# Mask and row maximum in one VectorE instruction, softmax weights scaled on VectorE, and two short query blocks in one PSUM bank, in the attention of the second of two transformer blocks

## What is computed

```python
def one_block(args):                       # one block of 128 queries
    ...
    score = jnp.where(admissible[None], score.astype(jnp.float32), -jnp.inf)
    _, sel = lax.top_k(score, k_sel)       # 128 keys for each query
    ...
    logits = (jnp.einsum('bqhr,bqkr->bqhk', ql, c_sel) * scale
              + jnp.swapaxes(bias, -1, -2))
    logits = jnp.where(valid[:, :, None, :], logits, -jnp.inf)
    p = jax.nn.softmax(logits, axis=-1)
    return jnp.einsum('bqhk,bqkr->bqhr', p, c_sel)
...
y = jnp.einsum('bsc,cd->bsd', jnp.concatenate([o_a, o_b], axis=-1), w_o)
x = _layer_norm(DEEPNORM_ALPHA * x + y, ln_g, ln_b)
```

## Time and profile before

| what | value |
|---|---|
| median of three runs | 1611.55 us (1610.61 to 1613.72) |
| the profiled execution | 1609.34 us, span of its instructions 1608.0 us |
| PE busy | 1540.8 us, 96% of the span |
| DVE, ACT, POOL busy | 992.7, 678.1, 194.0 us |
| mean granted TensorE clock | 0.985 |
| chain that ended last, by engine | PE 82%, DVE 9%, ACT 6%, POOL 2% |

### The profile page before, as it was taken

One profiled execution on the slowest core, in us unless ns is written; L12 is line 12 of the kernel. 1 busy time (PEld: TensorE's weight loads), 2 busy tenths in 40 slices (PEclk: granted clock), 3 DMA queues, 4 the chain that ended last, 5 costly groups with the idle time before them and its releaser, 6 DMA issues.

```text
span 1608.0 us, 18855 instructions
## 1 busy us (share of the span) xinstructions
PE 1540.8 (96%) x7486; PEld 1252.0 (78%) x7486; DVE 992.7 (62%) x1556; ACT 678.1 (42%) x1142; POOL 194.0 (12%) x176
## 2 busy tenths in 40 slices
PE   8999999999999999999989999999999998999797
PEld 6777878888888888677758888888888867886574
DVE  7466667966666656677764644434344489896444
ACT  6444444513232335455553522323243454556533
POOL 0000002000000012111103000000002005665211
PEclk9998999999999999999989999999999999999999
DMA  9334444566656632222212443333333203112011
GB/s 372 106 114 131 136 140 154 185 207 187 206 184 205 187 117 70 70 62 66 66 40 66 121 115 99 92 96 100 92 104 100 69 27 105 54 53 67 26 53 53
DMA packets 52171, 180.78 MB, mean 112 GB/s; under 512 B 5762, under 2 KB 6658, under 8 KB 52083
## 3 DMA queue, kind: packets, MB, share of 16 engines
q1 hardware_dynamic: 52082, 179.57, 35.4%
HBM read 176.01 MB, written 3.41 MB: 112 GB/s over the span
## 4 chain that ended last, share of the span: by engine, by line
PE 82%; DVE 9%; ACT 6%; POOL 2%; issue 1%; DMA 1%; SPq 0%; DVEq 0%; ACTq 0%
PE PS L481 22%; PE PS L484 22%; PE PS L482 22%; PE PS L491 2%; PE PS L494 2%; PE PS L492 2%; DVE sb_Wl L1486 1%; PE PS L718 1%; PE PS L537 1%; PE PS L823 1%; POOL sb_TMD L2092 1%; PE PS L737 1%; PE PS L631 1%; PE PS L556 1%; ACT sb_Wh L974 1%
## 5 line engine op out<-in xcount | busy, mean ns | idle before, releaser
L481 PE MATMUL PS<-sb_Hh,sb_Wh 128*128 128x512 f32 (+1 forms) x1016 | 407.2, 401 | 2.0 <-DVE sb_Hl L1517 2.0
L484 PE MATMUL PS<-sb_Hh,sb_Wl 128*128 128x512 f32 (+1 forms) x1016 | 397.8, 392 | 0.6 <-DVE sb_Wl L1486 0.6
L482 PE MATMUL PS<-sb_Hl,sb_Wh 128*128 128x512 f32 (+1 forms) x1016 | 397.8, 392 | 0.0
L974 ACT ACTIVATE sb_Wh<-sb_RAW 128x1024 fp32r<-128x1024 f32 x223 | 233.7, 1049 | 318.9 <-PE PS L484 312.1
L1486 DVE TENSOR_TENSOR sb_Wl<-sb_RAW,sb_Wh 128x1024 fp32r<-128x1024 f32 x223 | 285.9, 1282 | 92.4 <-ACT sb_Wh L974 92.4
L481 PE MATMUL PS<-sb_Oh,sb_Wh 128*128 128x512 f32 x672 | 265.4, 395 | 1.5 <-DVE sb_Ol L1568 0.9
L482 PE MATMUL PS<-sb_Ol,sb_Wh 128*128 128x512 f32 x672 | 262.5, 391 | 0.0
L484 PE MATMUL PS<-sb_Oh,sb_Wl 128*128 128x512 f32 x672 | 262.1, 390 | 0.0
L481 PEld LDWEIGHTS PS<-sb_Hh,sb_Wh 128*128 128x128 f32 (+1 forms) x1016 | 191.1, 188 | 59.4 <-issue 16.3
L484 PEld LDWEIGHTS PS<-sb_Hh,sb_Wl 128*128 128x128 f32 (+1 forms) x1016 | 190.7, 188 | 43.3 <-DVE sb_Wl L1486 1.0
L482 PEld LDWEIGHTS PS<-sb_Hl,sb_Wh 128*128 128x128 f32 (+1 forms) x1016 | 191.2, 188 | 40.2 <-issue 1.3
(11 more groups left out here) (348 smaller groups left out, 1989.0 us busy)
## 6 DMA issues: line engine op xcount, KB each, us to landing
sb_RAW<-w SPq DMA_DIRECT2D x128, 512.0 KB, 3.6
...
```

What stands on the lines that cost most here:

```text
L481: mm(to[0:m, :], WH[si][:, k, 0:m], hi[:, k, :], start=first, stop=False)
L482: mm(to[0:m, :], WH[si][:, k, 0:m], lo[:, k, :], start=False, stop=False)
L484: ins = mm(to[0:m, :], WL[si][:, k, 0:m], hi[:, k, :], start=False, stop=last)
L974: act(WH[slot_of(b)][:, :, 0:m], RAWS[raw_of(b)][:, 0:8 * m].rearrange("p (k m) -> p k m", k=8), ACT.Copy).then_inc(*done("w_hi", b))
```

## The change

1. **Logits** (DVE, `att_logits`): the product is scaled by -SCALE and the bias subtracted, so the row holds the negative logits. The mask has its sign turned (0 or +1e30). One instruction, `tensor_tensor_reduce`, adds it and takes the row's minimum, which is the negative maximum. POOL's mask addition and DVE's row maximum are gone. The exponential takes scale -1.
2. **Order on DVE and ACT**: the exponential of (h,3), (h,2) now stands in step 1, that of (h,1), (h,0) in step 2, each with mask, minimum, reciprocal and scaling. One slot sooner than before.
3. **Scaling** by the reciprocal is done by DVE (`att_weights`, a `tensor_scalar`), no more by ACT.
4. **Banks**: the logits of (h,1) and (h,0) share one bank of `G456`, with one semaphore for both. A head takes three banks instead of four.
5. **PB** has eight buffers: heads 0 and 1 of `Q` are added.
6. **PE in step 4**: both transposes stand ahead of `att_weigh(h, 3)`.

The core of the diff (left out: the mask of block 0, which turns its sign in the same way):

```diff
-        PB = Ring(sig, [x[:, h, :] for h in range(3) for x in (SH, vT)])
+        PB = Ring(sig, [x[:, h, :] for h in range(3) for x in (SH, vT)] + [Q[:, h, :] for h in range(2)])
...  (PE)
-                    to, free = G456.take(("lg", h, i), ("a_lg", h, i))
-                    e.wait_ge(at("a_ql", h), *free)
+                    if i:
+                        to, free = G456.take(("lg", h, i), ("a_lg", h, 0 if i == 1 else i))
+                        e.wait_ge(at("a_ql", h), *free)
+                    else:
+                        to = G456.buf(("lg", h, 1))[:, 256:384]
...
                 elif step == 4:
-                    att_weigh(h, 3)
                     att_turn(h, 1)
                     att_turn(h, 0)
+                    att_weigh(h, 3)
                     att_weigh(h, 2)
...  (ACT)
-                if step == 2:
-                    att_softmax(h, 3, 2)
+                if step == 1:
+                    att_exp(h, 3, 2)
+                elif step == 2:
+                    att_exp(h, 1, 0)
                 elif step == 3:
                     att_copy(h, 3)
                     att_copy(h, 2)
-                    att_softmax(h, 1, 0)
...  (DVE)
-                    stt(p[:, 0:L], G456.buf(("lg", h, i))[:, 0:L], SCALE, TBIAS[h][:, 384 - 128 * i:512], ALU.mult,
-                        ALU.add).then_inc(*done("a_lg", h, i))
+                    stt(p[:, 0:L], lg[:, 0:L], -SCALE, TBIAS[h][:, 384 - 128 * i:512], ALU.mult,
+                        ALU.subtract).then_inc(*done("a_lg", h, i))
+                    e.wait_ge(at("a_lg", h, i), at("mask", i))
+                    e.op.tensor_tensor_reduce(p[:, 0:L], p[:, 0:L], MK[i], 1.0, FILL_UP, ALU.add, ALU.min,
+                                              st[:, 4 * h + i, 0:1]).then_inc(*done("a_max", h, i))
+            def att_weights(h, *blocks):
+                for i in blocks:
+                    L, p, sl = 128 * (i + 1), PB.buf(("p", h, i)), st[:, 4 * h + i, :]
+                    e.wait_ge(at("a_exp", h, i))
+                    e.op.reciprocal(sl[:, 2:3], sl[:, 1:2]).then_inc(*done("a_rec", h, i))
+                    e.wait_ge(at("a_rec", h, i))
+                    ts(p[:, 0:L], p[:, 0:L], sl[:, 2:3], None, ALU.mult).then_inc(*done("a_p", h, i))
...
                 if step == 1:
                     att_logits(h, 3, 2)
+                    att_weights(h, 3, 2)
                 elif step == 2:
                     att_logits(h, 1, 0)
-                    att_softmax(h, 3, 2)
-                elif step == 3:
-                    att_softmax(h, 1, 0)
+                    att_weights(h, 1, 0)
...  (POOL)
-                    tt(p[:, 0:L], p[:, 0:L], MK[i], ALU.add).then_inc(*done("a_msk", h, i))
```

More of the change, by code:

```diff
@@ L1357, in rec_step, with att_exp @@
                     rows_rstd(("r", h), TA.buf(("rsq", h)), 128, "r_rs", h)
-            def att_softmax(h, *blocks):
+            def att_exp(h, *blocks):
                 for i in blocks:
@@ L2095, in rec_step @@
                         tt(S2[:, n, :], d[:, 0:128], S2[:, n, :], ALU.add).then_inc(*done("r_state", h, n))
-            def att_mask(h, *blocks):
-                for i in blocks:
-                    L, p = 128 * (i + 1), PB.buf(("p", h, i))
-                    e.wait_ge(at("a_lg", h, i), at("mask", i))
-                    tt(p[:, 0:L], p[:, 0:L], MK[i], ALU.add).then_inc(*done("a_msk", h, i))
             for n in range(38):
```

30 lines of the change are left out of this document (10 added, 20 removed).

## The result

| | before | with the change |
|---|---|---|
| median on the same chip | 1611.08 us (1609.31 to 1613.72, 4 runs) | 1593.93 us (1590.49 to 1597.23, 4 runs) |
| ratio to before, 95% interval | | 0.9903 [0.9876, 0.9931] |
| profiled execution, span | 1609.34, 1608.0 us | 1597.23, 1595.9 us |

The change makes the kernel about 1% faster; the ratio on record is 0.9903, the plain quotient of the two medians 0.9894. Four executions in all the runs of this document, of 1724.77 to 3090.78 us, stand far outside those of their kernels and are left out of every median and ratio.

What follows compares the result with a forecast made beforehand. PE, busy 96% of the span, was taken as the bound, gaining only where it idles or runs slow. Walking ticks 25 to 30 gave 14.2 us: 1611.55 - 14.2 = 1597.4 us, forecast 1594 to 1601 (0.55), range 1591 to 1604.

Steps and rivals of the forecast that it cites:

- The bound: PE from tick 25 to the output blocks: seven waits, 17.6 us, plus about 4.8 us of lower clock; ceiling 22 to 24 us.
- The walk: PE's tick starts worked out from tick 25 at 1467.4 to output blocks at 1526.5, before 1540.73: 14.2 us sooner.
- Tick 25: PE's 1.29 us wait goes because (1,2) takes the bank of (0,2); 0.43 + 2.14 + 5.46, tick 26 at 1475.4.
- Tick 26: PE waits 1.6 us for ACT's copies of the state products before logits (2,3); tick 27 at 1487.0, before 1488.9.
- Tick 27: ACT's output copy at 1490.3 plus 0.8 us for DVE beside POOL's chain; the 3.86 us wait goes; tick 28 at 1501.1.
- Tick 28: PE waits about 2.2 us instead of 1.37 for ACT's copy of head 0's result; tick 29 at 1513.6.
- Tick 29: PE waits 0.5 us; the earlier 5.33 us wait goes, since no softmax is left to do.
- Tick 30: PE waits 3.3 us for DVE's gate product, then 2.8 us for the rest at the lower clock; output blocks at 1526.5.
- DVE and ACT set the pace: Rival: costlier hand-overs or a 1.0 us fused instruction lengthen slots 25 to 28 by 1 to 1.5 us each; 1602 to 1606 us; 0.18.
- The fused instruction is slow: Rival: over twice the estimated time adds over 3 us across four slots, making each longer; 1615 to 1620 us; chance 0.05.
- The change does not remove its wait: Rival: another ring or semaphore holds (2,3) back, PE's waits stay, moved exponentials come on top; 1609 to 1614 us; chance 0.05.
- Nearly all waits go: Rival: ACT reaches its copies sooner, so ticks 26, 28 and 30 lose little; gain 17 to 21 us, 1591 to 1595; 0.17.

Runs made afterwards that it cites:

- the fastest version measured: Changed kernel with ACT's weight rounding before the exponentials (slots 24 to 27) and head 1's gate product and head 2's copy first in slot 30: 1587.54, again 1585.52 us.
- the ring alone: Kernel before the change with PB given eight buffers and one added wait on VectorE, nothing else: 1597.63 us, ratio 0.9931.

## Why the prediction was right

**The bound.** It said 17.6 us of waits and 4.8 us of clock, 22 to 24 us to be had. The stretch has 17.9 us of idleness (the 0.36 us of line 1373 were not in its rows), and PE is busy 4.9 us longer in it than with the change at the full clock. The account was right, and the fastest version measured took 20.0 us of it.

**The walk, slot by slot**, from tick 25: predicted 8.0, 11.6, 14.1, 12.5 and 12.9 us, measured 8.15, 11.35, 13.33, 12.47 and 11.94. The sum was 59.1, measured 57.24 in one profile and 59.69 in the other; before it was 73.35. The slots with a fully granted clock repeat to 0.02 us, so the differences can be laid to terms:

- Tick 25: logits and block take 7.71 us (1472.19 to 1479.90), not the 7.60 of their two terms.
- Tick 26: predicted a wait of 1.6 us for ACT's copy of the states, measured 1.20. PE came 0.15 us later, and the exponentials of (1,3) and (1,2) ended 0.3 us sooner after the tick's start than in the walk, with fused instructions of 0.69 us and not 0.75. The experiment with a bank for each logits shows that this wait and the 1.29 us of tick 25 are one and the same debt.
- Tick 27: the step that failed. It added 0.8 us of contention to the copy of the output, which made a wait of about 1.4 us. POOL's chain did become longer, but PE never waited for it: the wait was 0.35 us, the copy's own time behind PE's products. The rows on POOL:

```profile
1484.58 0.73 POOL L2096 TENSOR_SCALAR sb_TMD<-sb_CB,sb_dec 128x128 f32<-128x128 f32 x1 [19.74 <-ACT sb_CB L1351]
...
1487.99 0.95 POOL L2099 TENSOR_TENSOR sb_CB<-sb_TMD,sb_CB 128x128 f32<-128x128 f32 x1
...
1492.35 0.51 POOL L2099 TENSOR_TENSOR sb_CB<-sb_TMD,sb_CB 128x128 f32<-128x128 f32 x1
```

  The chain lasts 1492.35 + 0.51 - 1484.58 = 8.28 us, against 7.75 before, and 7.5 us in the experiment with the mask on POOL, where DVE is idle beside most of it. So the chain grew by 0.5 to 0.8 us; the term had about the right size and the wrong place: PE's products of the states (line 867) show no wait, and ACT's copy follows them. The link of 0.95 us stands beside DVE's gate product (line 1987, 0.69 us from 1487.93), not beside the fused instruction. By the rule of the Trainium skill, page "SBUF — State Buffer", section "Who interferes with whom", an instruction of DVE with two SBUF inputs contends with a GpSimd instruction that reads SBUF. The row agrees in kind. The 0.6 us that the prediction took off its sum by that rule came to nothing, since the chain was not on the path.
- Tick 28: predicted 2.2 us for the copy of head 0's result, measured 0.87 for the bank of the row sums and 0.82 for the copy. The transposes in front of the multiplication fill part of it: in the old order the wait is 2.25 us.
- Tick 29: a wait of 0.5 us was predicted, none came.
- Tick 30: predicted 3.3 us for the gate product and a lower clock behind it, measured 2.96 us; behind it PE needed 1.65 us at the full clock in the first profile and 2.42 us in the second, where 2.8 were predicted. The old order would have saved 1.24 us of that wait (1.72 in its place), not 1.8.

So the waits that would be left in ticks 26, 28 and 30, their places and releasers were right (but for the row sums in tick 28). The two terms that put most of the 1.9 us too much into the stretch, contention and clock behind tick 30, are one misplaced and one that comes in some executions only. Of the 3.5 us between forecast and median, 0.5 are the median before, which was 1611.08 and not 1611.55, and the last 1.1 us are less than the spread of the four runs, 1590.49 to 1597.23: that the forecast came this near is in part luck.

**What the change is made of.** The prediction gave each part a term but no share. The runs give it: the ring alone 9.6 us, and the rest 6.5 us, for which mask and minimum must be on DVE (17.6 us lost without), the scaling too (10.1 us) and the eighth buffer must be there (13.0 us). Each of these losses holds both idleness (10.9, 5.8 and 7.5 us) and clock. The parts don't add up: with any one of the three taken back the stretch is longer (67.3 to 74.8 us) than with eight buffers and the old order (63.8 us). The fused instruction with the old order of the exponentials was not tried, so what the sooner exponentials are worth by themselves stays open.

**The rivals.** "DVE and ACT set the pace" was right as a mechanism: doubling the fused instruction lengthened two waits one for one. It did not decide, because the instruction is cheap. Its price for a fused instruction of 1.0 us, 1 to 1.5 us a slot, was not tested as such: doubling adds 2.1 us a slot, and slots 26 and 28 grew by 5.6 and 3.8 us, clock included, slots 25 and 27 not at all. Its case against, DVE's work under 9 us a slot, was a little low: 9.72 and 9.13 us in slots 26 and 27. "The fused instruction is slow" had a wrong sum: twice the estimate adds 2.2 us a slot, not over 3. Doubled, the kernel was still faster than before, 0.9971. "The change does not remove its wait" fell: no wait for logits is left. The advice of the Trainium skill, page "Perfetto Trace Analysis", section "Optimizing Scalar/DVE Operations", to offload work to ScalarE or GpSimd, is given for a saturated DVE. The stretch before was no such case, though the prediction let the rule stand for it: DVE was busy 36.93 us of 73.35 there and ACT 46.60, so the scaling went from the busier engine to the less busy one. Work moved back costs 10.1 us on ACT and, with the minimum apart, 17.6 us on POOL. "Nearly all waits go" did not happen in the change, though the median, 1593.93 us, lies in its 1591 to 1595 as well as at the edge of the forecast's 1594 to 1601: the waits tell the two apart and the time does not. Nearly all waits go in the last version.
